# Two row sums, two row normalisations and one table split change their places in the output stage of a stick-breaking and GLA layer kernel

## The reference

```python
    h = _rmsnorm(x, g_pre[layer]); proj = h @ w_in[layer]
    y_sb  = (stick_breaking(q, k, v) * silu(sb_z))  @ w_o_sb[layer]
    y_gla = (rmsnorm(gla_chunked(...)) * silu(gla_z)) @ w_o_gla[layer]
    gates = sigmoid(gate_logits + b_gate[layer])
    merged = gates[..., :D] * y_sb + gates[..., D:] * y_gla
    x = x + merged @ w_out[layer]
    return _rmsnorm(x, g_final)
```

## Time and profile before

| | us |
|---|---|
| median of 3 runs | 814.1 (813.5 to 814.67) |
| the profiled execution, its time | 813.5 |
| the profiled execution, its span | 811.8 |
| PE busy in the span | 791.7 (98%) |
| DVE busy in the span | 582.3 (72%) |
| ACT busy in the span | 410.1 (51%) |

### The profile page before, as it was taken

How to read it: one execution, slowest core, us unless ns; L and a number is a source line. 1 busy time by engine, 2 the same in 40 slices (tenths; PEclk the granted TensorE clock), 3 DMA queues, 4 the chain that set the end, 5 groups by cost and what they waited for, 6 DMA issues and landing times.

```text
span 811.8 us, 11845 instructions
## 1 busy us (share of the span) xinstructions
PE 791.7 (98%) x4441; PEld 662.7 (82%) x4441; DVE 582.3 (72%) x823; ACT 410.1 (51%) x706; POOL 30.4 (4%) x32
## 2 busy tenths in 40 slices
PE   6999999999999999999999999999999999999996
PEld 5778888887888888879889888888888888888885
DVE  6528896989698788865545655566457777779985
ACT  7536675666666566656235245244344343365442
POOL 1530000000000000020000000000000000000000
PEclk9999999999999999999999999999999999999999
DMA  9862012202120220021110011144443333395222
GB/s 322 285 206 52 27 30 49 52 26 63 41 52 26 52 52 27 27 72 54 33 52 27 1 40 39 65 144 155 142 143 105 103 104 104 105 359 211 104 105 103
DMA packets 72483, 76.31 MB, mean 94 GB/s; under 512 B 3804, under 2 KB 57207, under 8 KB 71928
## 3 DMA queue, kind: packets, MB, share of 16 engines
q1 hardware_dynamic: 72386, 75.71, 29.0%
q10 hardware_dynamic: 54, 0.01, 0.0%
HBM read 55.79 MB, written 15.73 MB: 88 GB/s over the span
## 4 chain that ended last, share of the span: by engine, by line
PE 83%; DVE 9%; ACT 3%; issue 3%; DMA 0%; DVEq 0%; ACTq 0%
PE pj L698 22%; PE tr L1002 5%; PE ob L950 5%; PE sc L950 5%; PE pj L842 4%; PE pj L1002 4%; PE ob L1002 4%; DVE surv L1671 4%; PE ob L790 3%; PE sc L1002 3%; PE pj L714 3%; PE tr L800 3%; PE pj L823 3%; PE tr L1060 2%; PE pj L1060 2%
## 5 line engine op out<-in xcount | busy, mean ns | idle before, releaser
L698 PE MATMUL pj<-h_hi,w_lo 128*128 128x512 f32 x336 | 134.2, 399 | 0.0
L698 PE MATMUL pj<-h_hi,w_hi 128*128 128x512 f32 x336 | 133.8, 398 | 0.0
L698 PE MATMUL pj<-h_lo,w_hi 128*128 128x512 f32 x336 | 133.7, 398 | 0.0
L1671 DVE TENSOR_TENSOR_SCAN surv<-surv 128x128 f32<-128x128 f32 (+3 forms) x64 | 86.5, 1351 | 19.2 <-ACT beta L1169 18.7
L698 PEld LDWEIGHTS pj<-h_hi,w_lo 128*128 128x128 f32 x336 | 63.5, 189 | 12.1 <-issue 0.5
L698 PEld LDWEIGHTS pj<-h_lo,w_hi 128*128 128x128 f32 x336 | 63.3, 188 | 12.1 <-issue 0.3
L698 PEld LDWEIGHTS pj<-h_hi,w_hi 128*128 128x128 f32 x336 | 63.5, 189 | 11.7 <-issue 0.2
L1210 ACT ACTIVATE wt_hi<-tr 128x512 fp32r<-128x512 f32 (+2 forms) x96 | 43.7, 490 | 43.2 <-PE tr L800 41.7
L1594 DVE TENSOR_TENSOR w_lo<-w_raw,w_hi 128x1024 fp32r<-128x1024 f32 x33 | 40.3, 1222 | 26.6 <-ACT w_hi L1102 26.4
L1716 DVE TENSOR_TENSOR wt_lo<-tr,wt_hi 128x512 fp32r<-128x512 f32 (+2 forms) x96 | 50.1, 549 | 5.3 <-ACT wt_hi L1210 4.8
L1674 DVE TENSOR_TENSOR beta<-beta,surv 128x128 f32<-128x128 f32 (+3 forms) x64 | 48.6, 759 | 2.2
(11 more groups left out here) (400 smaller groups left out, 1911.1 us busy)
## 6 DMA issues: line engine op xcount, KB each, us to landing
w_raw<-in_w_in SPq DMA_DIRECT2D x30, 512.0 KB, 3.7
y_scratch<-y_ring SPq DMA_DIRECT2D x28, 256.0 KB, 2.0
graw<-in_w_in SPq DMA_DIRECT2D x14, 512.0 KB, 4.7
y_back<-y_scratch SPq DMA_DIRECT2D x14, 512.0 KB, 5.2
x_t<-in_x SPq DMA_DIRECT2D x8, 512.0 KB, 6.1
wrow<-in_w_out SPq DMA_DIRECT2D x4, 1024.0 KB, 7.4
w_scratch<-wsum SPq DMA_DIRECT2D x4, 1024.0 KB, 4.6
wout_raw<-in_w_out SPq DMA_DIRECT2D x8, 512.0 KB, 7.5
```

What stands on the lines that cost most here:

```text
L698: mm = pe.matmul(pj[bank][:, :], (w_lo if p == 2 else w_hi)[:, slot, k, :], (h_lo if p == 1 else h_hi)[:, k, HALF * h:HALF * h + HALF], st ...
L1671: dve.tensor_tensor_scan(s[:, ::-1], s[:, ::-1], s[:, ::-1], 1.0, ALU.mult, ALU.bypass)\
```

## The change

On DVE, `row_sum(2)` and `row_sum(3)` move from around `item_sums(1, 1)` to behind `gather(4)` of pair 1. `norm_row(0, 0)` and `norm_row(1, 1)`, with the wait for `g_final`'s broadcast, move from behind `gather(2)` and `gather(3)` of pair 1 to between `gather(6)` and `gather(7)` of pair 1. On ACT, `high_tw(2)` moves from behind `square(0, 0)` to ahead of it. Nothing is added or removed; PE's and SP's lists are the same.

```diff
@@ ACT
             high_out(1, 6)
+            high_tw(2)
             act.wait_ge(fin_bc, 1)
             act.wait_ge(o5_free, 3)
             square(0, 0)
-            high_tw(2)
             act.wait_ge(o5_free, 4)
             square(1, 1)
@@ DVE
             low_tw(1, 2)
-            row_sum(2)
             item_sums(1, 1)
-            row_sum(3)
             low_tw(0, 4)
@@ DVE, in the loop over pairs
                 if n == 0:
                     low_out(1, 6, 6)
-                    dve.wait_ge(fin_bc, 1)
-                    norm_row(0, 0)
                 else:
                     next_low(0)
                     next_low(1)
                 gather(3, xa1, banks[1], xa1, ALU.add, 1)
                 if n == 0:
                     low_tw(2, 6)
-                    norm_row(1, 1)
                     gather(4, xb2, banks[2], xb2, ALU.add, 2)
+                    row_sum(2)
+                    row_sum(3)
                     next_low(0)
                     next_low(1)
                     next_low(2)
@@ DVE, in the same loop
                 next_low(5)
+                if n == 0:
+                    dve.wait_ge(fin_bc, 1)
+                    norm_row(0, 0)
+                    norm_row(1, 1)
                 gather(7, xa2, banks[2], xa2, ALU.add, 5)
                 next_low(6)
```

## The result

| | before | changed |
|---|---|---|
| median, us | 814.0 (813.5 to 814.67, 4 runs) | 826.84 (826.14 to 827.61, 4 runs) |
| ratio to before | | 1.0157, 95% interval 1.014 to 1.0175 |
| the profiled execution, its time | 813.5 | 828.09 |
| its span | 811.8 | 826.4 |
| PE busy in it | 791.7 | 794.6 |

The change costs 12.8 us. The two profiled executions lie 14.6 apart. 1.17 of this arose ahead of everything that the change touches: pair 1 began at 748.91 in place of 747.74. The other 0.6 fits the clock's part, which was at its largest in this execution (2.8 us, against 1.4 to 2.0 in the others).

The account below looks back on a forecast made before the run. PE, never pausing, was taken to bound the kernel. Stall 11.2 plus clock 2.2 gave 13.4 us on the profiled 813.5, 826.9, plus 0.6 to the median: 827.5 us, 1.6% slower; range 824.8 to 830.0.

Parts of the forecast that it names:

- PE has nothing to give back: Pair 1 on PE: PE never pauses, so the 4.0 us DVE gains before 761 bring nothing.
- The row sums late for ACT: ACT's squares wait for late row sums: `square(0, 0)` at 760.1, was 750.35; `item_sums(2, 0)` at 766.6, 3.0 late.
- The end of the second scaling: On DVE, the second moved normalisation's scaling ends at 777.5, where it ended at 761.24 before.
- The reload: SP stores, then reloads the place for pair 2: 7.5 to 8.0 us after the scaling, so `gather(1)` at 785.0 to 785.5.
- PE's stall: PE waits at the fifth product of pair 2 for `gather(3)`: 10.9 to 11.4 us, taken as 11.2.
- The clock: After the stall PE returns at the lower clock level: 2.2 us lost, bounds 0 and 3.3.
- Behind it: Pair 3's reload, with slack 3.8 us of which 0.33 is used up, and the end: no further delay.
- the reload doesn't count: Rival: loads in time, only DVE's own delay remains, a stall of 4.5 us; 818.6 us; chance 0.03.
- not slower: Rival: normalisations fit DVE's slack if the second scaling ends by 765.9, PE never waits; 814.1 us; chance 0.03.
- the stall without the clock: Rival: PE comes back from its stall at full pace, cost 11.2 us; 825.3 us; chance 0.10.
- the longer table load: Part of rival "more than the sum" (chance 0.12): table switch holds ACT 1.3 us longer; 828.8 us.
- The longer return of the clock: Part of rival "more than the sum" (chance 0.12): clock's return costs 3.3 us for 2.2; 828.6 us.

Follow-up runs that it names:

- e8: The changed kernel run again unaltered, beside e7 as its measure; 826.84 us, ratio to before 1.0165.
- e5: Kernel before with only the two normalisations moved, to behind the first three low parts of pair 2 (`low_out(2, 2)`); 814.04 us.
- e3: Changed kernel plus 40 extra matmuls into a free bank on PE, directly ahead of its wait at the fifth product of pair 2; 824.32 us.
- e1: Kernel before with only the two normalisations moved to between `gather(6)` and `gather(7)` of pair 1; row sums and `high_tw(2)` stay; 821.36 us.
- e2: Changed kernel with pair 2's residual rows loaded early into a place of their own, so no reload waits for pair 0's stores; 820.65 us.
- e6: Kernel before with only the two normalisations moved, to behind `gather(5)` of pair 1; 814.56 us.
- e7: Changed kernel plus a one-element root on ACT ahead of the first square, so the root's table loads early; 825.63 us.

## Why the prediction was right, point by point

Forecast 827.5, measured 826.84; the sum was 13.4, the medians differ by 12.8. Times of the changed kernel in this list are less 1.17.

- **PE has nothing to give back.** Right. Of the 4.0 us that DVE gained before 761, 1.2 went to the row sums in their new place and most of the rest to idles for PE (0.21 and 1.40); it was ready for the low parts only 1.1 earlier, and its idle of 4.18 turned this into 3.1 late.
- **The row sums late for ACT.** `square(0, 0)` at 760.1 forecast, 760.2 measured (761.37); `item_sums(2, 0)` at 766.6 forecast, 766.7 measured.
- **The end of the second scaling.** 777.5 forecast, 777.6 measured. PE did not wait at the first product of pair 2, as forecast. That product has one more wait, which the prediction does not name: it needs the bank of a late row sum (`o5_free` at 4). The row sum ended at 761.87 and the product began at 767.79, so there was room.
- **The reload.** The one duration that was off: 7.5 to 8.0 forecast, 7.2 measured (778.77 to 785.96), 7.4 in e8. The nearer row of before, 7.5, was the better choice. In the changed kernel both parts were short: 2.7 us from the scaling to the reload's issue and 4.4 to its landing, where pair 3 of before had 3.5 and 4.0, and pair 2 of before 2.8 and 5.3. Over the runs the whole went from 7.2 to 8.8 (e5), so no single number was to be had.
- **PE's stall.** 11.2 forecast; the weight load that was at 777.27 stood at 789.10, 10.7 later when corrected. 0.5 too much, all of it from the reload; in e8 the load stood at 788.61, 10.9 later when corrected by that execution's own 0.48 (its pair 1 began at 748.22), 0.3 too much.
- **The clock.** 2.2 forecast from the pace at the kernel's start. The slow product and what follows it took 5.49 + 5.81 in the changed kernel, against 3.03 + 5.44 in e3 where the clock never fell: 2.8. In e8 the same product took 4.43, a loss of 1.4 only, and in e1 1.8. By e3 the medians say 2.5. The price is not the same in two executions of one kernel: those of e8 took 826.17 and 826.46 where the mean granted clock was 0.993, and 827.22 and 828.58 where it was 0.989. So 2.2 lies in the middle of what was seen, and all of it within 0 to 3.3. Part of this is luck: the 2.2 was carried over from transposes at another place, at half pace for 4.4 us, while here the matmuls ran at 0.43 in place of 0.227 for some 3 to 6 us of work.
- **Behind it.** No further wait, as forecast.
- **Wrong beside the sum.** The rival "the reload doesn't count" calls a stall of 4.5 us too short for the clock to fall and gives 818.6. e2, which makes that case, had this stall, but its clock fell and it measured 820.65. And in "not slower" the bound on the scaling's end, 777.27 less 3.2 less 8.0, is 766.1 and not 765.9; with the 7.2 that was measured it is 766.9, and e6, where it ended at 768.03 (767.5 when corrected by its start), had an idle of 0.3. Neither touches the forecast.

So the mechanism and its order were right and two terms were off: the stall 0.3 to 0.5 too long, the clock by 0.6 too short in the profiled execution and 0.8 too long in e8. Of the rivals, the stall without the clock is out by e3, the reload that does not count by e2, and the longer table load by e7. The longer return of the clock, 3.3, was not seen; 2.8 was the most.

## What to carry to other kernels

A step that nothing on its own engine waits for may still be the first link of a transfer: before a normalisation, a store or any last use of a buffer is moved later, follow the buffer to its reload and to the engine that reads it, and compare the landing, not the step, with the time of its use. Here the scaling could move by some 3 us for nothing (e5) and some 6 for an idle of 0.3 us (e6), and cost one for one from there on. And where an engine that sets the time never pauses, making a neighbour lighter can only move its idle; the price of a stall of this engine is its length plus what the clock takes, here 1.4 to 2.8 us for idles of 4.5 us and more, and nothing for idles of 0.3 and 1.4.

## What the runs showed of the hardware

The clock's part did not grow with the stall: 1.5 us for an idle of 4.5 (e2), 1.8 for 4.9 (e1), 2.0 for 9.2 (e7), and 2.8 and 1.4 for 10.3 and 10.5 (the changed kernel and e8). The fall came at different points: in e1 between 780 and 781, some 2 us after PE stopped, and in e2 only between 782 and 783, as PE was about to start again:

```profile
780.00:781.00 1.00, 0.00 (x0) 0.00 (x0) 1.00 (x2) 0.00 (x0) 0.00 (x0) 0.56 0.00 0
```
```profile
782.00:783.00 1.00, 0.28 (x1) 0.28 (x2) 0.96 (x4) 0.00 (x0) 0.00 (x0) 0.75 0.00 0
```

(the first row is e1, the second e2). PE then worked between about 3 us (e8: 788.6 to the stretch from 791 to 792) and 6 us (the changed kernel) at the lower level before it rose. Idles of 0.3 and 1.4 us (e6, e3) did not bring it down. And two stores with two reloads behind them into the same place, 512 KB each, took 7.2 to 8.8 us from the end of the scaling ahead of them to their landing, with the same list on SP.
